# One ScalarE table set for the exponentials and logarithms of the stick-breaking heads

## The reference, cut to what matters

```python
z = jnp.einsum('bhqd,bhkd->bhqk', qb, k).astype(jnp.float32) * scale
mask = kpos[None, :] < tq[:, None]
log_rem = jnp.where(mask, jax.nn.log_sigmoid(-z), 0.0)
suffix = lax.cumsum(log_rem, axis=3, reverse=True) - log_rem
a = jnp.where(mask, jnp.exp(jax.nn.log_sigmoid(z) + suffix), 0.0)
return jnp.einsum('bhqk,bhkd->bhqd', a, v).astype(q.dtype)
```

## Time and profile before

| | |
|---|---|
| time, median of 3 runs | 2390.54 us |
| the three runs | 2386.04, 2390.54, 2396.28 us |
| the profiled execution's own time | 2395.65 us |
| its span | 2393.7 us |
| PE busy | 2237.4 us, 93% of the span |
| ACT busy | 775.3 us, 32% |
| DVE busy | 1098.6 us, 46% |
| POOL busy | 87.5 us, 4% |
| mean granted TensorE clock | 0.957 of full speed |
| the chain that ended last, by engine | PE 83%, DVE 8%, ACT 6%, issue 2% |
| the stick-breaking heads | from 1815.84 us (scores of head 0) to 1917.46 us (first matmul of `out2`) |

### The profile page before, as it was taken

The page is one execution under the profiler, slowest core; times in us unless marked ns, Lnnn a source line. Parts: engine busy times, 40 slices in busy tenths (PEclk is TensorE's granted clock), DMA queues, the critical chain, the costliest instruction groups (busy, mean ns, idle before and its releaser), DMA issues.

```text
span 2393.7 us, 25076 instructions
## 1 busy us (share of the span) xinstructions
PE 2237.4 (93%) x10572; PEld 1765.8 (74%) x10572; DVE 1098.6 (46%) x1550; ACT 775.3 (32%) x1149; POOL 87.5 (4%) x84
## 2 busy tenths in 40 slices
PE   6997899999994999999999999899988898999999
PEld 4665678888873888888888888777755576888887
DVE  3637755555428433333533333453474346443421
ACT  3314432222223322222322222322455735322211
POOL 0000000000001000000111100100000001111100
PEclk9999999999996999999999999899887998999999
DMA  7521146555520232332223223224100021323222
GB/s 257 188 87 62 57 137 193 177 194 184 177 96 18 90 104 88 101 97 92 93 93 101 90 97 99 67 80 124 37 1 1 1 72 35 106 89 106 85 96 83
DMA packets 190784, 236.59 MB, mean 99 GB/s; under 512 B 4096, under 2 KB 175392, under 8 KB 190544
## 3 DMA queue, kind: packets, MB, share of 16 engines
q1 hardware_dynamic: 189696, 230.42, 29.7%
q0 software_dynamic: 976, 4.57, 0.6%
HBM read 231.96 MB, written 2.10 MB: 98 GB/s over the span
## 4 chain that ended last, share of the span: by engine, by line
PE 83%; DVE 8%; ACT 6%; issue 2%; DMA 0%; POOL 0%; SPq 0%; DVEq 0%; ACTq 0%; POOLq 0%
PE ps L399 24%; PE ps L401 24%; PE ps L400 24%; ACT pr L608 2%; PE ps L995 1%; PE ps L845 1%; PE ps L465 1%; DVE pr L633 1%; PE ps L1976 1%; PE ps L579 1%; PE ps L646 1%; PE ps L681 1%; DVE wl L348 1%; PE ps L378 1%; PE ps L443 1%
## 5 line engine op out<-in xcount | busy, mean ns | idle before, releaser
L399 PE MATMUL ps<-xh,wh 128*128 128x512 f32 x1800 | 714.6, 397 | 48.2 <-DVE xl L691 26.9
L400 PE MATMUL ps<-xl,wh 128*128 128x512 f32 x1800 | 707.5, 393 | 0.0
L401 PE MATMUL ps<-xh,wl 128*128 128x512 f32 x1800 | 707.1, 393 | 0.0
L348 DVE TENSOR_TENSOR wl<-raw,wh 128x2048 fp32r<-128x2048 f32 (+1 forms) x170 | 379.0, 2230 | 496.5 <-ACT wh L336 496.5
L399 PEld LDWEIGHTS ps<-xh,wh 128*128 128x128 f32 x1800 | 341.7, 190 | 128.3 <-issue 24.8
L336 ACT CAST wh<-raw 128x2048 fp32r<-128x2048 f32 (+1 forms) x170 | 315.3, 1855 | 339.7 <-PE ps L401 271.4
L401 PEld LDWEIGHTS ps<-xh,wl 128*128 128x128 f32 x1800 | 341.3, 190 | 73.3
L400 PEld LDWEIGHTS ps<-xl,wh 128*128 128x128 f32 x1800 | 342.0, 190 | 72.0 <-issue 1.2
L401 PE MATMUL ps<-hh,wl 128*128 128x512 f32 x704 | 280.9, 399 | 0.0
L400 PE MATMUL ps<-hl,wh 128*128 128x512 f32 x704 | 277.4, 394 | 0.0
L399 PE MATMUL ps<-hh,wh 128*128 128x512 f32 x704 | 276.2, 392 | 0.0
(11 more groups left out here) (331 smaller groups left out, 1901.3 us busy)
## 6 DMA issues: line engine op xcount, KB each, us to landing
raw<-in_ffn_w SPq DMA_DIRECT2D x52, 1024.0 KB, 5.3
raw<-in_ada_w SPq DMA_DIRECT2D x42, 1024.0 KB, 5.2
raw<-in_ffn_wg SPq DMA_DIRECT2D x22, 1024.0 KB, 5.3
raw<-in_ffn_wu SPq DMA_DIRECT2D x22, 1024.0 KB, 5.3
raw<-in_ffn_w SPq DMA_DIRECT2D x16, 896.0 KB, 4.6
raw<-in_ffn_wd SPq DMA_DIRECT2D x16, 896.0 KB, 4.6
raw<-in_w_in SPq DMA_DIRECT2D x10, 1024.0 KB, 5.2
raw<-in_ffn_wd SPq DMA_DIRECT2D x8, 1024.0 KB, 5.0
```

The lines of the kernel that those rows point to most:

```text
L348: e.tensor_tensor(wl[s][:, 0:n], r[:, 0:n], wh[s][:, 0:n].bitcast(F32), ALU.subtract).then_inc(*WLO.up(i))
L399: e.matmul(dst, ah, bh, start=start, stop=False)
L400: e.matmul(dst, ah, bl, start=False, stop=False)
L401: return e.matmul(dst, al, bh, start=False, stop=stop)
```

## The change

In slot NN, ahead of the logs of head 0, ACT is told to load the set `natural_log_exp_and_others`, which has both the exponential and the logarithm. The build step that places the loads then finds both functions in the set in place.

```diff
@@ -2079,6 +2079,8 @@
                 if s < NN:
                     act_exp(e, nsa_[s])
                 elif s < NN + 8:
+                    if s == NN:
+                        e.preload_act_table_set("natural_log_exp_and_others")
                     act_stick_logs(e, s - NN)
                 if 0 < s <= NN:
                     act_turn(e, nsa_[s - 1])
```

## The result

| | before | changed |
|---|---|---|
| median | 2391.63 us (7 runs) | 2378.16 us (7 runs) |
| range of the runs | 2386.04 to 2396.28 | 2369.55 to 2382.49 |
| ratio, 95% interval | | 0.9942 [0.9928, 0.9957] |
| span of the profiled execution | 2393.7 us | 2376.3 us |
| ACT busy | 775.3 us | 757.1 us |

The changed kernel is 0.58% faster, by 13.5 us. The forecast was 16.7 us and 2373.8; the measured time lies in the range. The two profiles, though, differ by 17.4 us in span and by 18.7 in the stretch that the change touches, more than the medians do.

A forecast was written before the change was run, and what follows sets the result against it. PE was taken as the bound, busy for 93% of the span, so ACT savings count only where PE stands still. 1.28 + 2.85 + 4.69 + 4.92 + 1.28 + 1.68 = 16.7 us off 2390.54 gave 2373.8, range 2367 to 2382.

The forecast's parts named there:

- The one load left: Ahead of head 0's scores: hidden in ACT's 3.51 us wait, cost 0, at most 1.28 us.
- Head 0: Load between exponential and logarithm goes, so PE's wait shortens: gain 1.28 us; up to 1.0 more kept for the range.
- Head 1: Three loads go from ACT's path; PE's whole idle time before head 2's scores is gained: 2.85 us.
- Heads 3 to 6: Pause of 1.23 us per head goes, PE paces at 8.68 instead of 9.91 us: gain 4.92 us.
- Head 2: Without the pause ahead the clock does not fall; head takes 8.68 instead of 13.37 us: gain 4.69 us.
- Behind head 7: Pause ahead of the last sums shrinks from 2.01 to 0.73 us: gain 1.28; full clock in the sums: 1.68.
- off the median: In the sum: the 16.7 us gain was subtracted from the runs' median, 2390.54 us, not the profiled 2395.65.
- the full count of the loads: Rival: all 15 loads count in full, as something paces PE together with ACT; 2364.9 us, chance 0.04.
- slower functions: Rival: the joint set's functions take longer in each head's chain; at twice their time about +8 us, 2398.5; chance 0.02.
- a longer switch: Rival: a switch also holds the next activation back, in head 0 and at the end; gain 19.3 us, 2371.2; chance 0.02.
- a set that is switched again between the heads: Rival: the set is switched again at run time, so the change does nothing; 2390.5 us, chance 0.02.
- The clock rival: Rival: clock falls all the same in head 2 or behind head 7; gain 10.3 to 15.0 us, chance 0.18.

The follow-up runs named there:

- before_c: The kernel before, unaltered, third profile: 96.60 us from the first scores of head 0 to the first matmul of the projection.
- again_b: The changed kernel, unaltered, third profile: ratio 0.9938 of before, median 2377.07 us, stretch from first scores to projection 82.90 us.
- one_ln: Changed kernel with one load put back between exponential and logarithm in heads 2 to 7, six in all: 0.9942 of before.
- before_b: The kernel before, unaltered, second profile: 96.61 us from the first scores of head 0 to the first matmul of the projection.
- one_second: Changed kernel with one load put back ahead of the second exponential in heads 1 to 6, six in all: 0.9935 of before.
- all_joint: Changed kernel with the joint set loaded again at each of the 16 places where before had a load: 1.0008 of before.

## Why the prediction came out as it did

The range and the direction held; the size was 16.7 for a measured 13.5, and in the repeats 14.4 and 14.5. Against the first two profiles the steps gave 2.41, 3.36, 4.77, 5.21 and 2.97 us (head 0, head 1, head 2, heads 3 to 6, behind head 7), 18.7 in all, and the forecast of 16.7 would have been too small. With before_c and again_b for the two kernels:

- **The one load left** at no cost: right. It ran at 1816.04, and ACT still waited 1.59 us for the scores behind it.
- **Head 0**, 1.28: measured 14.04 - 12.22 = 1.82, with 0.5 of the 1.0 that was kept for the clock. The clock was up again by the product, which took 1.95 us instead of 3.09, and PE then waited for DVE's copy, which the forecast had as free (again_b):

```profile
1824.67 1.95 PE L681 MATMUL ps<-pt,v2s 128*64 128x256 f32 x16
1827.60 2.42 PE L1976 MATMUL ps<-qsT,ksbT 64*128 64x512 f32 x8 [0.98 <-DVE pt L672]
```

- **Head 1**, 2.85: measured 2.92. PE goes from the product straight to the scores, and the rest of the three loads' 3.85 us buys nothing, as forecast.
- **Heads 3 to 6**, 4.92: measured 40.33 - 34.42 = 5.91. PE is the bound, at 8.61 and not 8.68 us, which gives 1.30 a head; the other 0.7 are heads 4 and 6 of before_c, which had the lower clock for a while and took 10.25 and 10.26 us; in the first trace they did not.
- **Head 2**, 4.69: **this step failed.** It took the 13.37 us of one execution for what the kernel takes. Two more profiles have 10.4, and against them the gain is 1.8. Of it 1.30 is the loop through ACT, which the first profile hid, and 0.5 the clock.
- **Behind head 7**, 1.28 for the load: measured 1.27. The 1.68 for the clock failed in the same way: 20.65 - 19.38 leaves nothing for it. It comes and goes; the first profile and one_ln paid it.

The sum is 1.82 + 2.92 + 1.78 + 5.91 + 1.27 = 13.7 us. The sentence that was wrong is "off the median". The profiled execution lay 5.1 us above the median of the three runs, and its stretch is 101.62 - 96.61 = 5.0 us longer than that of before_b, by the clock alone. Much of the two clock terms, 6.4 us, was thus probably missing from the median already, and the sum took it off again. That the forecast came within 3.2 us all the same has an element of luck: heads 0, 1 and 3 to 6 gave 1.6 us more than forecast, and made up for part of it.

Of the rivals, the full count of the loads is refuted by one_second and one_ln, slower functions and a longer switch by the rows of the joint set, and a set that is switched again between the heads by the single load in the trace. The clock rival's span of 10.3 to 15.0 holds the result, but not by its mechanism: the changed kernel's clock was full in head 2 and behind head 7 in all three profiles. What was smaller than forecast is what before had lost to the clock. The signs that were named for a wrong forecast, heads 2 to 6 over 9 us at a clock of 1.00 or a clock below 1 in head 2, did not appear in them.

## What to carry to other kernels

A table load is worth removing only as far as the engine that paces the stretch stands idle for it: fifteen loads were 19.2 us of ACT and gave about 14, and six of them put back where the pacing engine covers them cost 0.1. Split an expected gain into idle time and clock, and take the clock part from several profiles of one kernel, not from one; where the profiled execution lies above the median, look first whether that excess is the term that you are about to subtract. A pause of PE in front of dense work can be filled with matmuls that nothing reads; with two pauses filled the runs were 7.5 us shorter by the means (2377.3 to 2369.7), of which the places where it was done account for 4.5.

## What was not expected of the hardware

A low clock is nearly free as far as PE's pauses take up the extra work, and costs its full length where there are none: at a mean of 0.83 a head of before took 0.34 us longer, a head of the changed kernel 1.65. Past the pause it costs in before too: at 0.64 head 2 took 13.37 us against 9.91. So removing pauses also removes a cushion.

The same pause did not always bring the clock down. Behind the 2.01 us ahead of the last sums it fell in before's first profile and in one_ln, and not in before_b, before_c or all_joint; and heads 4 and 6, behind pauses of only 1.23 us, had the low clock for a while in before_b and before_c and not in the first profile of the same kernel. The Trainium skill (TensorE: Matmul & The Clock Gate, Part 1: The HAM clock gate) says that the moment at which the clock changes is not tied to the kernel and differs from run to run. The traces agree in part. One kernel's stretch took 101.62 us and then 96.61 and 96.60. But before_b, before_c and all_joint agree head for head to 0.02 us, so the low stretches came at the same places of the work in three executions on three chips; what makes it the one pattern or the other stays open.
